# Expert routing of a two-layer decoder step: five modulation tiles behind the row transposes, picks in three operations, sums over the other token tiles as products

## The reference, cut to what matters

```python
logits = h @ w_router + b_router
top_v, top_i = lax.top_k(logits, 2)
gates = softmax(top_v)
y = sum over e of comb[..., e] * swiglu(h, w1[e], w3[e], w2[e])     # comb: the two gates at the picked experts
x = x + gate2 * y
```

## Time and profile before

| | |
|---|---|
| median of 3 runs | 1671.34 us (1670.86 to 1680.17) |
| the profiled execution | 1675.75 us, its span 1674.0 us |
| PE busy | 1548.1 us, 92% of the span |
| PEld busy | 1463.9 us, 87% |
| DVE, ACT, POOL busy | 477.0, 371.9 and 416.6 us |
| mean granted clock of PE | 0.971 of full speed |
| chain that ended last | PE 87%, DVE 5%, DMA 3%, SPq 2%, issue 2%, ACT 1%, POOL 1% |

### The profile page before, as it was taken

One profiled execution on the slowest core, in us unless ns is written; L12 is line 12 of the kernel. 1 busy time (PEld: TensorE's weight loads), 2 busy tenths in 40 slices (PEclk: granted clock), 3 DMA queues, 4 the chain that ended last, 5 costly groups with the idle time before them and its releaser, 6 DMA issues.

```text
span 1674.0 us, 26732 instructions
## 1 busy us (share of the span) xinstructions
PE 1548.1 (92%) x11956; PEld 1463.9 (87%) x11956; DVE 477.0 (28%) x804; ACT 371.9 (22%) x622; POOL 416.6 (25%) x224
## 2 busy tenths in 40 slices
PE   7699989999999999999998975999999998999992
PEld 4399879899999999998997954999999988999992
DVE  1457662500111011226986231011110110010115
ACT  2321252322221222223225221111111110010114
POOL 0358135332343334424923302000000000000005
PEclk9899999999999999999999997999999998999995
DMA  7646242554343332333534083879789793748644
GB/s 234 190 130 174 76 126 82 176 168 127 86 124 119 101 101 61 104 125 104 156 97 126 6 288 128 274 272 323 244 270 330 271 306 117 247 151 303 221 140 176
DMA packets 291576, 286.76 MB, mean 171 GB/s; under 512 B 8109, under 2 KB 283199, under 8 KB 291414
## 3 DMA queue, kind: packets, MB, share of 16 engines
q1 hardware_dynamic: 203286, 230.23, 41.8%
q10 hardware_dynamic: 84400, 42.51, 9.2%
q0 software_dynamic: 3760, 12.09, 1.9%
HBM read 266.45 MB, written 19.07 MB: 171 GB/s over the span
## 4 chain that ended last, share of the span: by engine, by line
PE 87%; DVE 5%; DMA 3%; SPq 2%; issue 2%; ACT 1%; POOL 1%; POOLq 0%; ACTq 0%; DVEq 0%
PE PP L783 36%; PE PP L1109 22%; PE PP L1121 11%; PE PP L824 7%; PE PP L796 3%; PE PP L757 2%; PE PP L768 1%; DMA adaw<-in_w_ada 1%; PE PP L1080 1%; PE PP L1091 1%; DVE mem L1584 1%; DVE mem_r L1578 1%; PE PP L957 1%; DMA mem<-in_w_ada 1%; SPq L508 1%
## 5 line engine op out<-in xcount | busy, mean ns | idle before, releaser
L783 PE MATMUL PP<-hT_r,mem_r 128*128 128x260 f32 x2624 | 435.4, 285 | 4.6 <-DVE xT L1596 3.2
L639 POOL TENSOR_TENSOR mem_r<-mem,mem_r 128x1024 fp32r<-128x1024 f32 (+1 forms) x108 | 317.8, 2959 | 471.6 <-ACT mem_r L1237 471.2
L1109 PE MATMUL PP<-big,mem 128*128 128x144 f32 (+2 forms) x2816 | 375.2, 296 | 13.2 <-issue 12.4
L1109 PEld LDWEIGHTS PP<-big,mem 128*128 128x128 f32 x2816 | 372.9, 192 | 14.1 <-issue 12.8
L783 PEld LDWEIGHTS PP<-hT_r,mem_r 128*128 128x128 f32 x2624 | 363.7, 188 | 11.6 <-issue 7.7
L783 PE MATMUL PP<-mem_r 128*128 128x260 f32 x1312 | 263.8, 283 | 0.0
L783 PEld LDWEIGHTS PP<-mem_r 128*128 128x128 f32 x1312 | 201.8, 188 | 0.0
L1121 PE MATMUL PP<-big,mem 128*128 128x144 f32 (+2 forms) x1408 | 193.5, 294 | 0.0
L1121 PEld LDWEIGHTS PP<-big,mem 128*128 128x128 f32 x1408 | 186.6, 190 | 0.0
L739 POOL DMA_INDIRECT mem<-y_by_expert,place x10 | 9.5, 949 | 617.2 <-SPq L586 614.4
L824 PE MATMUL PP<-adaw,cs 128*9 128x128 f32 x1280 | 148.3, 274 | 14.0 <-DMA adaw<-in_w_ada 9.1
(11 more groups left out here) (237 smaller groups left out, 1064.9 us busy)
## 6 DMA issues: line engine op xcount, KB each, us to landing
mem<-in_w_moe SPq DMA_DIRECT2D x48, 1536.0 KB, 8.7
mem<-in_w_moe SPq DMA_DIRECT2D x32, 1408.0 KB, 8.8
adaw<-in_w_ada ACTq DMA_DIRECT2D x80, 512.0 KB, 5.0
mem<-in_w_dense SPq DMA_DIRECT2D x20, 1024.0 KB, 5.4
mem<-in_w_in SPq DMA_DIRECT2D x16, 1024.0 KB, 5.6
mem<-in_w_moe SPq DMA_DIRECT2D x16, 1024.0 KB, 7.0
mem<-in_w_dense SPq DMA_DIRECT2D x16, 704.0 KB, 4.7
mem<-in_w_out SPq DMA_DIRECT2D x8, 1024.0 KB, 5.1
```

The lines of the kernel that those rows point to most:

```text
L639: pool.tensor_tensor(r_(raw), raw, read_(hi), ALU.subtract).then_inc(w_lo, 1)
L783: mm = pe.matmul(PP[q][:, h, 0:HT], r_(w[:, k, :]), r_(x[:, k, HT * h:HT * h + HT]), start=(i == 0 and w is wh and x is hi), stop=(i == le ...
L1109: mm = pe.matmul(PP[w][:, f % 2, 0:n], raw[:, w, k, :], hn[:, k, 0:n], start=(k == 0), stop=(k == KD - 1))
```

## The change

Tile 75 leaves the place ahead of the router, tiles 76 and 77 leave the place after the third row transpose; all three stand with 78 and 79 after the fifth, behind the counting products. The ten one-hot operations of DVE become two over all token tiles and one that clears the rows that are not there, in the last token tile. The product with ones is issued first and raises `pre` by itself; then each token tile's place in the expert is accumulated on PE, the triangular product of its own picks and a product with ones for each earlier token tile (5 and 10 products), and `pre` is raised a second time. DVE no longer copies the two results or adds up the running sums; it adds the first rows to the PSUM result once.

```diff
-                 + [(("norm", 3), 4), (("route", 0), 2), (("route", 1), 2)]):
+                 + [(("norm", 3), 3), (("route", 1), 5)]):
...
-            pe.matmul(PP[0][:, 0, 0:NT * NE], tri[:], mflat, start=True, stop=True)
             pe.matmul(PP[0][:, 1, 0:NT * NE], ones[:], mflat, start=True, stop=True).then_inc(R["pre"], 1)
+            for t in range(NT):
+                own = PP[0][:, 0, t * NE:(t + 1) * NE]
+                mm = pe.matmul(own, tri[:], mask[:, t, :], start=True, stop=(t == 0))
+                for u in range(t):
+                    mm = pe.matmul(own, ones[:], mask[:, u, :], start=False, stop=(u == t - 1))
+            mm.then_inc(R["pre"], 1)
             for t in range(3, NT):
                 h_rows(t)
             ada_fill("route", 1)
...
+            experts = eidx[:].unsqueeze(1).to_broadcast([P, NT, NE])
             for r in range(2):
-                for t in range(NT):
-                    last = dve.tensor_scalar(pick[:, r, t, :], eidx[:], imf[:, t, r:r + 1], valid[:, t:t + 1],
-                                             ALU.is_equal, ALU.mult)
+                last = dve.tensor_tensor(pick[:, r], experts, imf[:, :, r:r + 1].to_broadcast([P, NT, NE]), ALU.is_equal)
             link(last)
+            link(dve.tensor_scalar(pick[:, :, NT - 1, :], pick[:, :, NT - 1, :], valid[:, NT - 1:NT], None, ALU.mult))
             dve.tensor_tensor(mask[:], pick[:, 0], pick[:, 1], ALU.add).then_inc(R["mask"], 1)
 
             dve.wait_ge(R["pre"], 1)
-            dve.tensor_copy(before[:], PP[0][:, 0, 0:NT * NE].rearrange("p (t e) -> p t e", t=NT))
-            dve.tensor_copy(totals[:, 1:NT, :], PP[0][:, 1, 0:(NT - 1) * NE].rearrange("p (t e) -> p t e", t=NT - 1))
...
             dve.tensor_copy(first[:], ebase[:]).then_inc(R["count"], 1)
-            link(dve.tensor_copy(totals[:, 0, :], ebase[:]))
-            for t in range(1, NT):
-                link(dve.tensor_tensor(totals[:, t, :], totals[:, t, :], totals[:, t - 1, :], ALU.add))
-            link(dve.tensor_tensor(before[:], before[:], totals[:], ALU.add))
+            dve.wait_ge(R["pre"], 2)
+            link(dve.tensor_tensor(before[:], PP[0][:, 0, 0:NT * NE].rearrange("p (t e) -> p t e", t=NT),
+                                   ebase[:].unsqueeze(1).to_broadcast([P, NT, NE]), ALU.add))
```

More of the change, by code:

```diff
@@ L194, in trunk_program @@
         before = sb("before", [P, NT, NE])
-        totals = sb("totals", [P, NT, NE])
         tri = sb("tri", [P, P])
```

## The result

The changed kernel takes 1679.33 us in the median of 20 runs, the kernel before 1671.94 us in as many: the ratio is 1.0031, with a 95% interval of 1.0016 to 1.0046. One run of the changed kernel took 5568 us and is left out of the ratio; the quotient of the two medians is 1.0044. By the ratio the change makes the kernel 5.2 us slower, less than one per cent, where 9.4 us faster was forecast. The profiled execution took 1679.53 us, its span 1677.7 us.

The account below looks back on a forecast made before the run. PE, at 87%, was taken to bound the kernel, its routing standing in a 6.5 us DMA gap. Row transposes 5.2 us earlier plus clock 4.2 us gave 9.4 us, from the median 1671.34 to 1661.9 us; range 1654 to 1672.

Parts of the forecast that it names:

- behind the rows: Before the row transposes: moved tiles and additions end last, at 1023.8, 0.9 us behind the rows read back at 1022.9.
- the picks are hidden but needed once the tiles are gone: Router stage: 1.5 us saved on DVE is hidden by PE's transposes; old picks would give the mask at Z + 5.4.
- the 22.8 I made of it: Scatter to DRAM: places at 996.5, first bytes 998.9, then 14.4 us plus 6.0 for other loads, landing at 1019.3.
- row transposes at 1023.8: Ahead of the experts: row transposes start at 1023.8 instead of 1029.03, 5.2 us gained.
- The clock step: Row transposes and first expert: clock up because tiles 78 and 79 run just ahead; 1.9 + 2.3 = 4.2 us gained.
- carried to the end: Experts: the 9.4 us gain lasts to the end, since experts wait on PE and their first six loads are there.
- The slower one that I priced, tile 79 later than 1024.3: Rival before the row transposes: tile 79's load lands at 1026, transposes 2 us later than before, 1673.2; chance 0.08.
- the late places: Rival in the routing: router and thirty passes at half clock, places at 1004.8, only the clock's 4.2 us stay; chance 0.06.
- my low-clock rival: Rival at tile 79 and row transposes: the clock stays down, gain only 3.7 us, 1667.6; chance 0.21.

Follow-up runs that it names:

- The shift alone: Kernel before with 28 small transposes more in the prologue, so PE's later code lies 55 instructions further, nothing else; 1.0036 of the kernel before.
- both causes mended: Changed kernel with nine register loads moved between tiles 77 and 78 and experts' code back at its old place modulo 256; 0.9960 of the kernel before.
- the kernel with five products: Changed kernel, register loads between tiles 77 and 78, experts' code at its old place, five counting products instead of fifteen; 0.9952 of the kernel before.
- the two with one mend each: Changed kernel with only the register loads moved between tiles 77 and 78 (1.0010), or only the experts' code back in place (1.0007), against the kernel before.
- the kernel with the loads moved: Changed kernel with PE's nine register loads of expert counts moved from behind the last modulation tile to between tiles 77 and 78; 1.0010 of the kernel before.

## Why the prediction was wrong

*Where it held.* Set off for the 2.9 us ahead of tile 72, the router ended at 986.6 (forecast 987.0), the places came at 995.8 (996.5), DVE waited 1.49 us for the second result (1.5), tile 78 got its weights at 1014.5 (1016.5), the tiles and DVE's additions were done at 1021.6 (1023.8), and behind the rows (1019.1, forecast 1022.9), as said. That the picks are hidden but needed once the tiles are gone is seen in the kernel with the tiles alone, where PE waits 0.99 us for the mask. The scatter, from places to landing, took some 19 us instead of 16.8, less than the 22.8 I made of it. Two readings of the clock column were a little off: the clock fell at 980.6, not 980.8, and rose at 1038.6, not 1038.3, which makes 0.15 us in the sum.

*The step that failed first* is "row transposes at 1023.8": I let them begin as soon as DVE's additions were done. Between these two PE executes nine register loads, 6.1 us, which no busy row shows and which had lain in the wait for the rows. The change takes that wait away. I put the loads at nothing, because I had not listed what the wait covered. The row transposes began 1.2 us earlier relative to tile 72 (56.4 us instead of 57.6), where 5.2 was forecast.

*The clock step* followed from it. The transposes ran at half clock as before, since the clock fell inside the hole; the experts did run at full clock from the first product on (1029.46), so 2.5 of the 4.2 us came. Even these are not all the change's: the kernel before took 132.9 us from tile 72 to expert 1, with its code 55 instructions further 129.2, 212 further 132.4, and the kernel with the picks and sums alone 132.0. So with the tiles in their old places the stage varies by 3.7 us.

*The step that failed second* is "carried to the end". I costed the thirty passes by their time and not as instructions ahead of some 49,000 others. The shift alone costs 0.36% (0.19 to 0.53), 6 us, about as much as the change lost. At three places of the code, in twelve kernels, the idle times lie ahead of the same experts: with the old place on 5 and 6, with 55 or 56 instructions more on 3, 4, 5, 6 and 7, with 212 on 5 and 6, with the one ahead of 5 cut from 9.3 to 9.8 us to about 3.5. The jumps to experts 3, 4 and 7 of the changed kernel, and that to expert 5 of the kernel before with its 9.3 to 9.8 us, lie at places 227, 15, 1 and 3, within 16 behind or 30 ahead of a multiple of 256; all those to experts of the usual width that began in time lie at 59 to 215. This rule was read off the late starts afterwards; one of them was foretold by it, the pause ahead of expert 5 in the kernel before with its code 212 further (about 3 us, measured 3.50). Experts 5 and 6, of other widths, begin at least 2.2 us late wherever the code lies; why, no run here shows.

That the missing code is being fetched in these idle times is not shown outright, but the traces come close. The profile has an instruction queue, q8, which in the changed kernel moved 110 packets with 1.80 MB, 16.4 KB a packet; within an expert one comes every 14 to 19 us. In all twelve kernels a packet of it ends 1.6 to 2.4 us before the first product of every late expert, and none in between; in the changed kernel, for instance, at 1233.97 us for expert 3, which begins at 1236.18. In the pause of 9.83 us ahead of expert 5 in the kernel before (1377.1 to 1386.9 us) no packet begins until 1382.4, and then there are two (packets, MB, share of 16 engines' time):

```profile
q8 instruction: 2, 0.03, 2.5%
```

So PE goes on when a packet of instructions has come; which instructions it holds the traces do not say. The Trainium skill (Runtime: NRT & Kernel Launch, "Instruction fetch mechanics") says that instructions come in blocks of 256 and that a taken branch out of the blocks at hand has to wait for its target's block. The period of 256, the idle times behind jumps and the packets that end in them agree with it.

*The rivals.* The slower one that I priced, tile 79 later than 1024.3, did not happen; the late places did not either. (In the first of these the sum was off: three loads at 5.9 us each take 17.7 us, not 20.) None of mine had a mechanism outside the stage. With both causes mended the change gives 6.7 us (4.2 to 9.2), between my low-clock rival (3.7) and the forecast (9.4). So the sum within the stage was near; what failed is what I took as given: that nothing else of PE's lay under the wait, and that the experts take the same time wherever their code lies.

## What to carry to other kernels

Before work is moved into a wait of an engine, list everything that the wait already hides on that engine, with the instructions that have no busy row: register loads, branches, semaphore waits. Where a long program jumps between bodies, as here, instructions added ahead of them can have a price of their own; compare two versions with the code at the same place modulo 256, or a difference like the 6 us here is put down to the wrong edit. And the place can also be used for a gain: look in the timeline for idle time with no releaser ahead of the bodies, and move the code.

## What the runs showed of the hardware

The clock fell at about 991.3 us in the changed kernel while PE's busy column stood at 1.00, towards the end of the thirty passes of 8 columns:

```profile
990.00:991.00 1.00, 1.00 (x11) 1.00 (x10) 0.33 (x3) 0.00 (x0) 0.00 (x0) 1.00 1.07 339
991.00:992.00 1.00, 1.00 (x8) 1.00 (x9) 0.11 (x1) 0.00 (x0) 0.00 (x0) 0.65 1.10 353
992.00:993.00 1.00, 1.00 (x6) 1.00 (x5) 0.81 (x5) 0.00 (x0) 0.00 (x0) 0.50 1.09 357
```

The row transposes behind them took 3.41 us for 16 passes instead of 1.97 for the first 16. In the kernel with five products (1.04 us for eight passes) the clock stayed at 1.00:

```profile
988.00:989.00 1.00, 1.00 (x11) 1.00 (x11) 0.83 (x7) 0.56 (x1) 0.00 (x0) 1.00 1.02 342
```

The thirty passes alone do not bring it down. In the kernel with picks and sums alone they stand behind two modulation tiles (1001.5 to 1005.0 us), and the clock stayed at 1.00:

```profile
1004.00:1005.00 1.00, 1.00 (x11) 1.00 (x11) 0.00 (x0) 0.00 (x0) 0.00 (x0) 1.00 0.00 0
```

In the four kernels in which it fell (the changed one, the two with one mend each and the one with both), the thirty passes follow the row transposes of three token tiles, with no modulation tile between.

The nine register loads on PE took 6.1 us, 0.68 us each, about as long as three tiles of the modulation product at 1.91 us, and the profile has no busy row for them.

A pause of PE costs more than its length where the clock falls in or behind it: 2.12 us ahead of expert 3 in the changed kernel were followed by 3.4 us at half clock, 1.7 us more. It does not always fall: in the kernel with the loads moved a pause of 2.26 us at the same place left the clock at 1.00.
